# Two transformer blocks on one core: norm weights applied at the split, a first chunk in portions, other places for a few waits

## The reference, cut to what matters

```python
def rmsnorm(x, g):
    xf = x.astype(jnp.float32)
    y = xf * lax.rsqrt(jnp.mean(xf * xf, axis=-1, keepdims=True) + EPS)
    return (y * g.astype(jnp.float32)).astype(x.dtype)

h = rmsnorm(x, g_mix_norm[l])
proj = jnp.einsum('bsd,de->bse', h, w_in[l])
sb_q, sb_k, sb_v, fx_q, fx_k, fx_v, f_logit, m_q, gate_logit = split_columns(proj, SPLITS)
o_sb = stick_breaking_attention(...)      # q, k, v of "sb", 8 heads of 64
log_f = jax.nn.log_sigmoid((f_logit + b_forget[l]).astype(jnp.float32)).transpose(0, 2, 1)
o_fox = forgetting_attention(fq, fk, to_heads(fx_v, FOX_HEADS, HD), log_f)
mh = rmsnorm(mem, g_mem_norm[l])
mkv = jnp.einsum('bmd,de->bme', mh, w_mem_kv[l])
o_mem = memory_attention(mq, mk, to_heads(mv, MEM_HEADS, MEM_HD))
merged = gates[:, :, 0] * br_sb + gates[:, :, 1] * br_fox + gates[:, :, 2] * br_mem
x = x + jnp.einsum('bsd,de->bse', merged, w_out[l])
# then a norm and a relu-squared MLP; the second block follows
```

## Time and profile before

| what | value |
|---|---|
| median of 3 runs | 1136.45 us |
| lowest and highest | 1135.9 and 1138.89 us |
| the profiled execution's own time | 1135.34 us |
| its span | 1133.5 us |
| TensorE busy | 1113.0 us, 98% of the span |
| VectorE, ScalarE, GpSimd busy | 627.2, 584.4, 136.1 us |
| moved by DMA | 184.34 MB, mean 163 GB/s |

### The profile page before, as it was taken

One profiled execution on the slowest core, in us unless ns is written; L12 is line 12 of the kernel. 1 busy time (PEld: TensorE's weight loads), 2 busy tenths in 40 slices (PEclk: granted clock), 3 DMA queues, 4 the chain that ended last, 5 costly groups with the idle time before them and its releaser, 6 DMA issues.

```text
span 1133.5 us, 14203 instructions
## 1 busy us (share of the span) xinstructions
PE 1113.0 (98%) x5899; PEld 933.9 (82%) x5899; DVE 627.2 (55%) x688; ACT 584.4 (52%) x906; POOL 136.1 (12%) x200
## 2 busy tenths in 40 slices
PE   6999999999999999999999999999999999999998
PEld 5777788887999988888878888888889788888887
DVE  5544554557645445457657665555457676555552
ACT  5688654443455534346567364444447655444431
POOL 1022111110132200032311000000004300000000
PEclk9999999999999999999999999999999999999999
DMA  9533343445554555545122255554544235555552
GB/s 338 209 127 133 149 145 116 149 173 196 197 190 180 193 186 186 192 154 186 59 96 91 75 186 186 186 185 167 186 149 147 95 124 191 192 180 187 184 169 74
DMA packets 28384, 184.34 MB, mean 163 GB/s; under 512 B 3472, under 2 KB 3856, under 8 KB 8080
## 3 DMA queue, kind: packets, MB, share of 16 engines
q1 hardware_dynamic: 26496, 177.52, 43.5%
q0 software_dynamic: 1824, 5.92, 1.6%
HBM read 182.38 MB, written 1.05 MB: 162 GB/s over the span
## 4 chain that ended last, share of the span: by engine, by line
PE 93%; ACT 3%; DVE 2%; DMA 1%; POOL 0%; issue 0%; SPq 0%; DVEq 0%
PE ps L577 23%; PE ps L580 23%; PE ps L579 23%; PE ps L557 6%; PE ps L692 4%; PE ps L672 3%; PE ps L610 3%; PE ps L609 3%; PE ps L608 3%; DVE t L1770 1%; ACT t L1191 1%; PE ps L904 1%; ACT t L1188 1%; DMA t<-in_w 1%; ACT L1188 1%; PE ps L661 1%
## 5 line engine op out<-in xcount | busy, mean ns | idle before, releaser
L1770 DVE TENSOR_TENSOR t<-t 128x2048 fp32r<-128x2048 f32 (+8 forms) x292 | 418.8, 1452 | 342.1 <-ACT t L1191 334.9
L1191 ACT ACTIVATE t<-t 128x2048 fp32r<-128x2048 f32 (+5 forms) x235 | 330.6, 1425 | 279.9 <-PE ps L580 243.2
L577 PE MATMUL ps<-t 128*128 128x512 f32 (+2 forms) x1186 | 469.1, 396 | 3.4 <-DVE t L1770 1.8
L580 PE MATMUL ps<-t 128*128 128x512 f32 (+2 forms) x1186 | 461.1, 389 | 0.0
L579 PE MATMUL ps<-t 128*128 128x512 f32 (+2 forms) x1186 | 460.6, 388 | 0.0
L577 PEld LDWEIGHTS ps<-t 128*128 128x128 f32 x1186 | 223.2, 188 | 47.1 <-DVE t L1770 4.3
L580 PEld LDWEIGHTS ps<-t 128*128 128x128 f32 x1186 | 223.0, 188 | 46.4
L579 PEld LDWEIGHTS ps<-t 128*128 128x128 f32 x1186 | 223.4, 188 | 43.3 <-DVE t L1770 0.8
L2458 POOL TENSOR_TENSOR t<-t 128x32 f32<-128x32 f32 (+8 forms) x108 | 91.1, 854 | 530.9 <-ACT t L1188 458.0
L1188 ACT ACTIVATE t<-ps,t 128x256 f32<-128x256 f32 (+4 forms) x216 | 95.9, 453 | 95.3 <-DVE t L1927 46.0
L557 PE MATMUL ps<-t 128*128 128x128 f32 (+3 forms) x667 | 96.8, 275 | 12.9 <-DVE t L1770 10.4
(11 more groups left out here) (97 smaller groups left out, 532.5 us busy)
## 6 DMA issues: line engine op xcount, KB each, us to landing
t<-in_w SPq DMA_DIRECT2D x158, 1024.0 KB, 4.9
t<-in_w SPq DMA_DIRECT2D x8, 512.0 KB, 3.6
t<-in_w SPq DMA_DIRECT2D x5, 768.0 KB, 4.3
t<-in_g POOLq DMA_DIRECT2D x6, 512.0 KB, 5.3
t<-in_w SPq DMA_DIRECT2D x2, 640.0 KB, 3.9
t<-in_x SPq DMA_DIRECT2D x4, 256.0 KB, 5.0
t<-in_mem POOLq DMA_DIRECT2D x1, 1024.0 KB, 11.0
out<-t SPq DMA_DIRECT2D x4, 256.0 KB, 4.8
```

Of the source, the lines that this page charges most:

```text
L577: e.matmul(o, sh, wh, start=k0 + j == 0, stop=False)
L580: t = e.matmul(o, sl, wh, start=False, stop=last and j == n - 1)
L1191: return e.activation(o, src, ACT.Copy, scale=scale)
L1770: return e.tensor_tensor(o, a, b, op)
```

## The change

- The norm weights of x and of the memory tokens are no longer spread rows (`G_MIX` and `G_MEM` go) but columns `gmix` and `gmem` of the constants, that land with the identity (`FIRST`). TensorE turns the raw tokens (`turn_raw`); the weight is applied as a per-partition factor at the split, in four instructions of 128 columns instead of one of 512 on ScalarE (hi) and on VectorE (lo) (`split_gained`). The hi part of x's second half of c=0 is made by VectorE.
- Chunk 0 is loaded in four portions of 256 KB with semaphores of their own. The second half of x (c=1) is loaded behind chunk 1. `gemm_first` does chunk 0 pass by pass: eight xhi*whi, then eight xhi*wlo, then eight xlo*whi.
- `warm`: two products of 512 columns and, after the turns of x c=0, two of 128, all of zeros in the scratch for squares, into bank 7, that nothing reads.
- x c=1 is turned between the halves of chunk 1, the memory tokens c=0 into banks 7 and 6, c=1 between the halves of chunk 6; the thin product uses bank 6.
- ScalarE does the squares of x c=0 ahead of cut 2 and those of c=1 behind it; the log forget gate is done for both halves in one instruction each; `stick_soft` no longer waits for the memory tokens' turns.
- `turn_fox` is divided by halves around `stick_sums`; the scores of FOX[0] go ahead of chunk 18 and its exponents ahead of the placing of the memory keys; the turn of the merged second half goes between the halves of chunk 37, and cut 39 behind its split.
- GpSimd's loads of the rows for the next two norms (`G_MLP`, `G_NSA`) no longer wait for the gains that used the buffers.

The diff, without small reorderings of the same kind:

```diff
@@ -79,7 +79,8 @@
-G_MIX, G_MEM, G_MLP, G_NSA, G_FF0, G_FF1 = range(6)
+G_MLP, G_NSA, G_FF0, G_FF1 = range(4)
+FIRST = 144
...
@@ -587,6 +588,28 @@
...
+    def gemm_first(x):
+        n, wd = CHUNKS[0][3:5]
+        _, whi, wlo = m.chunk(0)
+        js = [slice(j * wd, (j + 1) * wd) for j in range(n)]
+        pair = PAIRS["sbqk", 0]
+        o = [take(pair[h], "sbqk", 0, h)[:, 0:wd] for h in range(2)]
+        for j in range(n):
+            for h in range(2):
+                w.wait_ge(*after("hi of", "x", 0, h))
+                w.wait_ge(*after("hi", 0, j))
+                e.matmul(o[h], x(j, h)[0], whi[:, js[j]], start=j == 0, stop=False)
+        for j in range(n):
+            for h in range(2):
+                w.wait_ge(*after("lo", 0, j))
+                e.matmul(o[h], x(j, h)[0], wlo[:, js[j]], start=False, stop=False)
+        for h in range(2):
+            w.wait_ge(*after("off", "x", 0, h))
+            for j in range(n):
+                t = e.matmul(o[h], x(j, h)[1], whi[:, js[j]], start=False, stop=False)
+        t.then_inc(*summed(("used", 0)))
...
+    def turn_raw(tag, src, c, there, banks=(None, None)):
+        for h in range(2):
+            w.wait_ge(*after(*there(h)))
+            turn4((tag, c, h), src[:, h, col4(c)], 4, banks[h])
...
+    def warm(n, cols):
+        for i in range(n):
+            t = e.matmul(bank[7][:, 0:cols], m.sqx[:, 0:128], m.sqx[:, 0:cols], start=True, stop=True)
+        t.then_inc(*summed(("warm", cols)))
+    w.wait_ge(*after("zeros"))
+    warm(2, 512)
     w.wait_ge(*after("ident"))
     x, ready = normed("x")
-    turn_normed("x", 0)
-    gemm(0, x, ready)
-    turn_normed("x", 1)
-    for c in (1, 2, 3):
+    turn_raw("x", m.X, 0, lambda h: ("ld x", h, 0))
+    warm(2, 128)
+    gemm_first(x)
+    gemm(1, x, ready, (0,))
+    turn_raw("x", m.X, 1, lambda h: ("ld x", h, 1))
+    gemm(1, x, ready, (1,))
+    for c in (2, 3):
         gemm(c, x, ready)
     for h in range(2):
         w.wait_ge(*after("off", "sbqk", 0, h))
         turn4(("sb", 0, h), m.fxv[:, h, :])
-    thin(4, spare(), "x")
+    thin(4, 6, "x")
     gemm(5, x, ready)
...
         turn4(("sb", 1, h), m.stg0[:, h, :])
     for c in range(2):
-        turn_normed("m", c)
-    gemm(6, x, ready)
+        turn_raw("m", m.memx, c, lambda h: ("mem",), ((7, 6), (None, None))[c])
+        gemm(6, x, ready, (c,))
     w.wait_ge(*after("off", "flog"))
     for h in range(2):
         turn(("fl", h), [m.flt[:, half(h)]])
...
-    def turn_fox(b):
+    def turn_fox(b, h):
         w.wait_ge(*after("masks"))
-        for h in range(2):
-            v = heads(m.stg0[:, h, :], 66)
-            w.wait_ge(*after("off", "fx", b, h))
-            w.wait_ge(*after("cumulated", b, h))
-            for c in range(2):
-                turn(("fx", b, h, c), [v[:, 4 * c + j, :] for j in range(4)])
+        v = heads(m.stg0[:, h, :], 66)
+        w.wait_ge(*after("off", "fx", b, h))
...
@@ -785,14 +836,16 @@
     stick_values(0)
     stick_scores(1)
     gemm(10, x, ready)
-    turn_fox(0)
+    turn_fox(0, 0)
     stick_sums(1)
+    turn_fox(0, 1)
     gemm(11, x, ready)
     stick_values(1)
     stick_scores(2)
     gemm(12, x, ready)
-    turn_fox(1)
+    turn_fox(1, 0)
     stick_sums(2)
+    turn_fox(1, 1)
     gemm(13, x, ready)
...
@@ -803,30 +856,18 @@
     gemm(16, xm, ready_m)
     turn_heads("mq", 0, "mq")
     gemm(17, xm, ready_m)
+    fox_scores(FOX[0])
     gemm(18, xm, ready_m)
     turn_heads("mkv", 0, "mk")
...
@@ -861,10 +902,11 @@
     def ready(k, h):
         return after("off", "mg", k // 4, h)
-    gemm(37, merged, ready)
+    gemm(37, merged, ready, (0,))
     for h in range(2):
         w.wait_ge(*after("merged", 1, h))
         turn4(("mg", 1, h), m.mg[:, h, 512:1024])
+    gemm(37, merged, ready, (1,))
     gemm(38, merged, ready)
     gemm(39, merged, ready)
...
@@ -1221,6 +1263,15 @@
     def split_half(tag, c, h, buf=m.HT):
         split((tag, c, h), buf[0][:, 4 * c:4 * c + 4, half(h)])
+    def split_gained(tag, g, c, h, buf):
+        w.wait_ge(*after("on", tag, c, h))
+        p = bank(tag, c, h)
+        for j in range(4):
+            k = 4 * c + j
+            t = copy(buf[0][:, k, half(h)], p[:, j * 128:(j + 1) * 128], m.cst(g)[:, k:k + 1])
+        t.then_inc(*rounded(("hi of", tag, c, h)))
...
@@ -1263,15 +1314,18 @@
-    split_normed("x", 0)
+    split_gained("x", "gmix", 0, 0, m.HT)
     cut_by_piece(0)
     cut_by_piece(1)
+    w.wait_ge(*after("warm", 128))
+    for h in range(2):
+        square_sum(("x", 0, h), m.X[:, h, col4(0)], m.cols("ss", "x", 0, n=2)[:, h:h + 1])
     cut(2)
-    for c in range(2):
-        for h in range(2):
-            w.wait_ge(*after("ld x", h, c))
-            square_sum(("x", c, h), m.X[:, h, col4(c)], m.cols("ss", "x", c, n=2)[:, h:h + 1])
-    split_normed("x", 1)
+    for h in range(2):
+        w.wait_ge(*after("ld x", h, 1))
+        square_sum(("x", 1, h), m.X[:, h, col4(1)], m.cols("ss", "x", 1, n=2)[:, h:h + 1])
+    for h in range(2):
+        split_gained("x", "gmix", 1, h, m.HT)
     cut(3)
...
@@ -1294,24 +1348,21 @@
     for h in range(2):
         place(("sb", 1, h), m.sbk[:, :, half(h)])
     for c in range(2):
-        split_normed("m", c, m.mT)
+        for h in range(2):
+            split_gained("m", "gmem", c, h, m.mT)
     cut(8)
-    for h in range(2):
-        z, na, ex, l = (m.FT[:, h, 8 * i:8 * i + 8] for i in range(4))
-        w.wait_ge(*after("off", "fl", h))
-        act(na, z, ACT.Abs).then_inc(*out(("fl abs", h)))
-        w.wait_ge(*after("fl abs", h))
-        act(ex, na, ACT.Exp, scale=-1.0).then_inc(*out(("fl exp", h)))
-        w.wait_ge(*after("fl exp", h))
-        act(l, ex, ACT.Ln, bias=1.0).then_inc(*out(("fl ln", h)))
+    z, na, ex, l = (m.FT[:, :, 8 * i:8 * i + 8] for i in range(4))
+    w.wait_ge(*after("off", "fl", 1))
+    act(na, z, ACT.Abs).then_inc(*out(("fl abs",)))
+    w.wait_ge(*after("fl abs"))
+    act(ex, na, ACT.Exp, scale=-1.0).then_inc(*out(("fl exp",)))
+    w.wait_ge(*after("fl exp"))
+    act(l, ex, ACT.Ln, bias=1.0).then_inc(*out(("fl ln",)))
     for h in range(2):
...
     def stick_soft(p):
-        for h in range(2):
-            for c in range(2):
-                w.wait_ge(*after("on", "m", c, h))
...
@@ -1397,6 +1434,22 @@
+    cut(20)
+    exponents(FOX[0], m.P0)
...
@@ -1434,10 +1487,11 @@
     cut(36)
     for h in range(2):
         split(("mg", 0, h), m.HT[0][:, 4:8, half(h)])
-    for c in range(37, 40):
+    for c in range(37, 39):
         cut(c)
     for h in range(2):
         split(("mg", 1, h), m.o_sb[0][:, :, half(h)])
+    cut(39)
...
@@ -1805,9 +1859,18 @@
         for h in range(2):
             split_half(tag, c, h, buf)
-    def gain(tag, c, h, g, src=m.X):
+    def split_gained(tag, g, c, h, buf):
+        w.wait_ge(*after("hi of", tag, c, h))
+        p = bank(tag, c, h)
+        for j in range(4):
+            k = 4 * c + j
+            t = e.scalar_tensor_tensor(out=buf[1][:, k, half(h)], in0=p[:, j * 128:(j + 1) * 128], scalar=m.cst(g)[:, k:k + 1],
+                                       in1=buf[0][:, k, half(h)].bitcast(F32), op0=ALU.mult, op1=ALU.subtract)
+        t.then_inc(*rests(("off", tag, c, h)))
+    def gain(tag, c, h, g):
         w.wait_ge(*after("gain", g))
-        tt(m.tmpa[:, h, col4(c)], src[:, h, col4(c)], m.gB[:, g % 2, col4(c)], ALU.mult).then_inc(
+        tt(m.tmpa[:, h, col4(c)], m.X[:, h, col4(c)], m.gB[:, g % 2, col4(c)], ALU.mult).then_inc(
             *out(("gained", tag, c, h)))
     def reduce_heads(key, nh, n):
@@ -1823,44 +1886,41 @@
+    e.memset(m.sqx[:], 0.0).then_inc(*out(("zeros",)))
     w.wait_ge(*after("ident"))
     e.tensor_copy(m.identb[:], m.ident).then_inc(*out(("identb",)))
-    for h in range(2):
-        w.wait_ge(*after("ld x", h, 0))
-        gain("x", 0, h, G_MIX)
-    split_normed("x", 0)
+    w.wait_ge(*after("on", "x", 0, 1))
+    for j in range(4):
+        t = e.tensor_scalar(m.HT[0][:, j, half(1)], bank("x", 0, 1)[:, j * 128:(j + 1) * 128], m.cst("gmix")[:, j:j + 1],
+                            None, ALU.mult)
+    t.then_inc(*out(("hi of", "x", 0, 1)))
     cut_by_piece(0)
     for h in range(2):
-        w.wait_ge(*after("ld x", h, 1))
-        gain("x", 1, h, G_MIX)
+        split_gained("x", "gmix", 0, h, m.HT)
     cut_by_piece(1)
     cut(2)
-    split_normed("x", 1)
+    for h in range(2):
+        split_gained("x", "gmix", 1, h, m.HT)
     for c in range(3, 6):
         cut(c)
-    w.wait_ge(*after("mem"))
-    for c in range(2):
-        for h in range(2):
-            w.wait_ge(*after("on", "x", c, h))
-            gain("m", c, h, G_MEM, m.memx)
     w.wait_ge(*after("ld masks"))
...
     cut(7)
     for c in range(2):
-        split_normed("m", c, m.mT)
-    cut(8)
+        for h in range(2):
+            split_gained("m", "gmem", c, h, m.mT)
     r0 = m.cols("rms", "x", n=2)
     w.wait_ge(*after("rms", "x"))
     w.wait_ge(*after("consts"))
     for h in range(2):
```

(33 more changed lines are left out.)

106 lines of the change are left out of this document (56 added, 50 removed).

## The result

The changed kernel takes 1124.28 us in the median of four runs (1124.08 to 1124.9), the one before 1136.64 (1135.9 to 1138.89): a ratio of 0.9889, 95% interval 0.9872 to 0.9906. It is faster, by 12.4 us in the medians. The profiled executions stand 11.03 us apart (1135.34 and 1124.31), their spans 11.0 us; the steps are read in these. The forecast was 1126.0 us in a range of 1123.5 to 1130.5.

A forecast was written before the change was run, and what follows sets the result against it. TensorE was taken as the bound, busy 1113.0 of 1133.5 us, leaving 20.4 us idle and slow early products to win. Start 4.8 plus waits 4.95 gave 9.75 us off 1135.34, 1125.6; 1126.0 was said, range 1123.5 to 1130.5.

The forecast's parts named there:

- The start: Launch to first product of chunk 2: that mark moves from 25.74 to 20.9 us, 4.8 us gained (bounds 2.5 to 6.2).
- The waits behind it: TensorE's waits after the first product of chunk 2: removing them gains 4.95 us, 3.3 if covers fall short by a third.
- thin product: First window, 36 to 62 us: the thin product's wait of 0.25 us goes with its own bank.
- memory turns: Turns of memory tokens: waits of 0.34 and 1.01 us go, through free banks 7 and 6 and half of chunk 6.
- two waits at forgetting heads' turns: Turns at 88 and 106 us: 0.43 us goes twice, 0.86 in all, with `stick_sums` covering the copies.
- scores and exponents of FOX[0]: Wait at 153 us: 1.25 us goes, the exponents of 2.8 us lying under chunk 18's 5.5.
- merged second half, chunk 37, and all behind it: Wait at 282 us: 0.98 us goes under half of chunk 37.
- The edit priced at 0.26 us: Log forget gate and soft pass: of 0.58 us of waits, 0.26 goes as three ScalarE instructions and waits between halves fall away.
- The loads at chunk 2: Rival, 18 in 100: GpSimd's 2.7 MB delays chunk 2's landing to 17 to 19 us; total 1127.7 to 1129.7 us.
- The clock at 1.2 GHz through chunk 0: Rival, 12 in 100: chunk 0's products stay slow, gain about 7 us, total 1128.4 us.
- The waits come back elsewhere: Rival, 8 in 100: removed waits are paid where ScalarE is next behind; total 1132 us.
- Slower: Rival, 3 in 100: GpSimd's burst makes chunk 2 land last, after 28 us, for a loss of 3.4 us.

The follow-up runs named there:

- e3: Changed kernel with chunk 0 loaded in one piece of 1 MB instead of four portions of 256 KB: 1126.97 us.
- e7: Changed kernel with all four loads of x, second half included, ahead of the portions of chunk 0: 1126.44 us.
- e1: Changed kernel without its four products of zeros: 1125.54 us.
- e9: Changed kernel with chunk 0 in one load and sixteen small products of zeros instead of two behind the turns of x: 1125.5 us.
- e2: Changed kernel with the new start and log forget gate kept, the other edits to the later waits put back as before: 1133.16 us.
- e6: Changed kernel with only the thin product's bank and the memory turns (chunk 6 whole behind them) put back as before: 1129.58 us.
- e12: Changed kernel with only the log forget gate by halves again and VectorE's cut 8 ahead of it, as before: 1130.4 us.
- e8: Kernel before with its own start and log forget gate, only the places of the later waits changed: 1133.49 us.
- e4: Changed kernel with ScalarE splitting x's second half before it squares it: 1124.54 us.
- e10: Changed kernel with x's second load issued first from ScalarE's queue instead of SyncE's: 1124.13 us.
- e5: Changed kernel with GpSimd's two loads of norm rows issued behind its factor of x: 1124.88 us.

## Why the prediction was right

**The total** was right: 1126.0 said, 1124.28 measured, inside the range and inside the likeliest case's own 1124 to 1127.5, near its lower end. "Faster by over 0.3%" (0.91) came true. That it came so near is in part luck: the gain of the start was put 0.55 us too high and that of the waits 1.8 us too low.

**The start.** First turn near 5 us: 4.71. First product near 8.1: 8.08. Zero product at four passes, 1.7 us, the pair by 4.9: 1.8 each where the clock stays low (3.58 for both in e3), and the pair was done by 4.71 here. Four instructions of 128 columns, 1.1 to 1.2 us: 1.14 and 1.12. Portions there by 8.6: ScalarE works on them from 7.31 with no wait until it has done four, and the last one, issued at 3.52, landed 5.8 us later, at 9.3. Chunk 0 ended near the forecast's 13.8, with chunk 1 from 14.22. First product of chunk 2 at 20.9 with a wait below 1 us ended by VectorE: 21.32, 0.59 us idle, ended by VectorE (L1867). The prediction's chain for it, the landing of chunk 2 plus 5.9 us, is the one that the trace shows: 15.0 + 5.9 = 20.9 was said, 15.71 + 5.61 = 21.32 measured. So the landing was 0.7 us too early and the work behind it 0.3 too long. The 4.8 us became 4.25, of which 0.17 is the two views' difference at the old mark. Not foreseen: x's second load let its turns start only at 6.17 instead of near 5, an idle stretch of 0.86 us between the turns. The sum gave each part of the start no price of its own; the runs do: the portions 3.0 us (e3), the load order 3.7 in the profiled execution and 2.2 by the medians (e7), the zeros 0.34 (e1, at the mark), or 1.6 where a load is late (e9 against e3). These do not add up: each is the loss without one part, and portions and order act on the same first landing and the same clock. Nor would a still earlier chunk 0 bring anything: TensorE already waits for what hangs on chunk 2's landing.

**The waits behind it.** All seven went as said, and the term "Sum: 0.25 + 0.34 + 1.01 + 0.86 + 1.25 + 0.98 + 0.26 = 4.95" was mis-sized: 6.75 measured.

| edit | said | measured (table of starts) |
|---|---|---|
| thin product | 0.25 | 0.49 |
| memory turns | 1.35 | 1.95 |
| log forget gate, soft pass | 0.26 | 0.48 |
| two waits at forgetting heads' turns | 0.86 | 1.32 |
| scores and exponents of FOX[0] | 1.25 | 1.21 |
| merged second half, chunk 37, and all behind it | 0.98 | 1.43 |

The mark to the turns of "sb" 0 lost 0.13, and with it the rows add up to 6.75. Most of the 1.8 us too little (1.2 of it) is one error: idle time was taken for the price of a wait, though each shown wait leaves 0.16 us or so in the modelled end of the instruction before it. By the distances of the starts the waits of the earlier trace rows are 5.9 us instead of 4.7, 0.41 + 0.50 + 1.27 + 0.59 + 0.60 + 1.43 + 1.14; e2 and e6 bear it out.

**The edit priced at 0.26 us** was right as a term and wrong as a reading. Alone it can gain little, since the wait it ends is one of 0.17 us (no run has it alone); without it the kernel loses 4.1 us (e12, mark taken off), of which by its own timeline the wait is 2.68, its modelled end some 0.2 and seven slow products about 1.4. "Three ScalarE instructions and the waits between halves fall away" left out two loads of tables, 2.6 us, that stand in the trace of before. The forecast held because this edit was in the change, which is luck and not the reading's merit.

**The rivals.** *The loads at chunk 2*: its mechanism is real, since the mark hangs on that landing (5.61 us behind it in six executions), but its size is not: 15.71 and not 17 to 19. *The clock at 1.2 GHz through chunk 0*: no; pass one takes 2.49 us for eight products, paced by ScalarE's four pieces (2.64 us), and passes two and three are 0.23 apart. e3 and e7 show what it takes, waits of 3.17 and of 1.75 and 1.08 us. *The waits come back elsewhere*: not in this kernel, but in e8 and e12, where half of the change brings it about. *Slower*: nothing of it seen.

**The medians against the profiled executions.** The medians are 12.4 us apart and the profiled executions 11.0. The kernel before, e2, e8 and e12 have long waits and spread by 1.9 to 4.4 us; the changed kernel's runs by 0.8. The mean granted clock of each execution goes with this: in the changed kernel it is 1.000 in three and 0.998 in the one of 1124.9 us; in e6 1.000 at 1127.44 us and 0.998, 0.998 and 0.997 at 1129.41, 1129.76 and 1129.96; in e12 it goes from 0.998 at 1128.83 us down to 0.993 at 1133.26. A mean of 0.998 is a loss of 0.002 x 1126 = 2.3 us of full clock, an estimate that fits e6's 2.0 to 2.5. So with the same waits the clock falls in some executions and not in others, and a kernel with fewer waits is spared it more often. Behind which wait it fell in an execution that was not profiled stays open, and so does how much of the 1.4 us between the two differences is this and how much the scatter of the landings.

**The sum of e8.** At the thin product and the memory turns 0.51 + 1.94 us are gained; 1.24 are lost in chunk 0, 1.68 at the forget gate's wait and 1.6 by the clock behind it. At the first sums of stick heads 0.52 come back, because the wait of 0.41 us that stands there in the kernel before (71.09) is covered by the delay. The later places bring 3.9. Together 2.4, as measured.

## What to carry to other kernels

Price a wait by the distance of the starts on both sides of it less the work between them, not by the idle time shown, and look at the granted clock of the other executions too: e6 costs 3.1 us in its profiled execution and 5.3 by the medians. Before a wait is taken away, follow the next place where the helper engines are behind, with each load of activation tables counted: a wait is often what lets them catch up, and a gain of 2 us was given back 7 us later until that place was mended too. At a cold start, the first bytes count more than the rate: a small first load, ahead of everything that is not needed for it, was worth 3 us, more than the products of zeros gave. And follow a wait back past the engine that ends it: the one at chunk 2 is ended by VectorE and moves with a load, to a hundredth of a microsecond.

## What the runs showed of the hardware

- TensorE's clock can fall behind waits of a few microseconds in the midst of work: behind 3.17 us (e3), 1.75 and 1.08 with two products between (e7), 1.84 (e8) and 2.68 (e12) came seven to fourteen products of 512 columns at 0.43 us instead of 0.23, the 1.2 GHz level. In e8 and e12 this came only 2 to 3 us after the wait, behind small instructions that were still fast. In the profiled executions it did not fall behind 1.96 and 0.38 us (e6, e2), 1.61 (e6, at 7.87) or 1.23 (e4, at 8.00), nor behind 0.86 and 0.80 us at the changed kernel's start; but three of e6's four executions show a lower mean granted clock. A wait of about 2 us can so cost another 1.5 us that stand as busy time.
- In e3 the turns and zero products ahead of the long wait were still 0.21 us apart. That the clock was up in between is read from the granted clock, 1.00 from 8 to 10 us and 0.66 from 10 to 15, and from e10, where the same spacing is followed by a fast chunk 0 when the wait is only 0.29 us. The granted clock alone does not show a slow start: it stands at 1.00 also where the first products of the kernel before are 0.43 apart.
- With the same two products of zeros from 1.44 us on, the time at which the clock rises differs: the eight turns were fast from 4.71 (the changed kernel), slow and then fast (1.31 us, e4) or slow to the end (1.91 us from 5.02, e3), and without zeros the slow level lasted until about 11.8 (e1).
- A float32 product of 512 columns costs 1.8 us at the 1.2 GHz level (3.58 for two, e3), about four times the 0.43 of the reduced form.
- The landing of the same load scatters by 1 us between kernels whose start is the same: chunk 2 at 15.46 (e6) to 16.44 us (e5), and the mark with it.
